# Second mixer of a two-block transformer: attention by head pairs at longer distances, masks on TensorE, two result banks, the whole convolution on VectorE, the output product begun early

## The chip, the core and the metric

The kernel runs on one core of a Trainium2 chip, in one launch. The metric is the time of one execution on the device in microseconds, the median over several runs. [...]

## The reference, cut to what matters

T = 256 rows, D = 1024. A first block of two layers (feed-forward, a mixer of three kinds of attention, feed-forward) is unchanged in what it computes. Behind it come two layers of this:

```
def hybrid_layer(x, ...):
    h = rms_norm_2(x, norm_g)
    z = h @ w_in
    (fq, fk, fv, ff, f_gate, glu_in, c_gate,
     nq, nkc, nvc, nks, nvs, nkw, nvw, n_gl, n_gate) = jnp.split(z, split_points, axis=-1)
    o_a = fox_attention(heads(fq, FOX_HEADS), heads(fk, FOX_HEADS),
                        heads(fv, FOX_HEADS), ff + fox_b) * jax.nn.silu(f_gate)
    o_b = conformer_conv(glu_in, conv_w, conv_b, conv_ln_g, conv_ln_b,
                         conv_pw) * jax.nn.silu(c_gate)
    o_c = nsa_attention(heads(nq, NSA_HEADS), ...) * jax.nn.silu(n_gate)
    mixed = jnp.concatenate([o_a, o_b, o_c], axis=-1)
    return x + mixed @ w_out
```

`fox_attention` has 4 heads of 64 with a decay on the scores (a running sum of log-sigmoids of `ff`). `conformer_conv` gates 256 channels by a sigmoid, runs a causal convolution of 31 taps on each channel, a layer norm over channels, a Silu and a 256 x 256 product. `nsa_attention` has 8 query heads on 2 key groups and three branches: compressed keys (15 blocks, each the result of a small network with a Gelu), selected keys and window keys; at T = 256 the selected and the window branch are both plain causal attention, with their own keys and values. The last layer is followed by a norm.

## The kernel before, in words

**Products.** A fp32 product is three products of rounded halves: with `whi`, `wlo` the high and the low part of a weight and `hh`, `hl` those of the normed input, `mm3` issues the three on PE at L301, L302 and L303. Other products and score terms go through `mm` (L306), transposes through `tr` (L311). A class `Stream` brings the weights in the order of a plan, a chunk of 128 x 1024 at a time: DMA into one of four `raw` buffers, ACT rounds it to `whi` (L261), DVE subtracts to get `wlo` (L265), both issued when the chunk's place among the split buffers comes free.

**Banks.** The eight PSUM banks are given out by rings: MM (0 to 2) for projections, SB (3, 4) for scores, TB (5, 6) for transposes, OB (7) for the sum over values, WB (0 to 4 and 7) for row products.

**A layer of the second mixer** (`mixer2`, L1108; layer 1 at 1337.8 to 1560.3 us of the trace, layer 2 from 1560.3 us on):
- Three row products of the input, each over eight 128-row slices of the depth: `nq`, `nkv` (512 columns) and `n3` (284 columns: fox values and small gates); then a rotation on DVE and `turn_n` (transposes of queries and keys, split into `qTh`, `qTl`, `kTh`, `kTl`).
- `weave(side(), 100, main, 44)` (L1647) interleaves two generators on one instruction stream. `main` is `tiles()`: pairs of 128-column tiles of the projection ("col2", 24 products of 256 columns a tile) and the compression product `bank<-raw,bl`, in the order glu, compressed keys and values, fox queries and keys, compression, gates. `side` is the attention, 32 heads-by-branches of nsa and then 8 of fox, with small work in between: branch gates, fox decay, layer norm, `compressed()`, `gating()`.
- Attention takes heads two at a time for the scores (`scores_pair`, run by `run_pairs`): three or four products into a bank, then for each head a custom DVE instruction (L695) that adds the causal table, writes the scores to `wk` and keeps their least value, and an Exp on ACT (L326). Each head is then turned by transposes, copied to SBUF alternately by DVE (L323) and ACT (L314), and multiplied with the values into the single OB bank. After 8 heads `fin_nsa` scales that bank on DVE into `oc` (directly, or through `ntmp` and an addition).
- The convolution: channels 0 to 127 on POOL (`conv_pool`, a scale L334 and an addition L329 a tap), channels 128 to 255 on DVE (`conv_dve`, L337, one `scalar_tensor_tensor` a tap).
- Gates: six column tiles times the row norms into `rg` on DVE, one Silu pass late (`gating`), which multiplies the turned results into `hh`, `hl`; then `out_rows`, the output product with `w_out` over all of `hh`, `hl`, four banks, and the residual addition.

What sets the order on each engine is the order in which these generators are advanced; every engine then works through its own list in that order, waiting at each entry for its semaphores.

## Time and profile before

| what | value |
|---|---|
| median of 3 runs | 1780.35 us (1779.28 to 1781.01) |
| profiled execution | 1780.6 us |
| its span | 1778.8 us |
| PE busy | 1654.0 us, 93% |
| DVE busy | 988.1 us, 56% |
| ACT busy | 807.5 us, 45% |
| POOL busy | 222.8 us, 13% |
| second mixer, layer 1 | 222.5 us |
| second mixer, layer 2 and final norm | 218.5 us |

The profiled execution is 0.25 us above the median and its span 1.8 us shorter than its time. PE busy is close to the span in the first block; the two layers of the second mixer are the last 441 us. "Busy" adds up the durations of instructions, and matmuls overlap in them, so the share of a stage is to be read with the idle time and the clock beside it.

### The profile page before, as it was taken

What the parts mean: (1) busy time and instruction counts of PE and PEld (TensorE: products, weight loads), DVE (VectorE), ACT (ScalarE), POOL (GpSimd) and SP (SyncE); (2) the same over time, 40 slices, a digit from 0 to 9 for tenths busy, and PEclk for the clock granted to TensorE, in tenths of its full rate; (3) what the DMA queues carried; (4) which work ended last, traced back from release to release, by engine and by line L of the source; (5) the groups of instructions that cost most, each with busy time, mean ns of one, the idle gap of its engine ahead of it and who ended that gap; (6) DMA issues with size and microseconds to landing.
All of it is one profiled execution on the core that took longest, in us unless ns stands there. A gap on an engine that the chain in (4) does not pass through costs nothing.

```text
span 1778.8 us, 24856 instructions
## 1 busy us (share of the span) xinstructions
PE 1654.0 (93%) x9598; PEld 1440.0 (81%) x9598; DVE 988.1 (56%) x1532; ACT 807.5 (45%) x1270; POOL 222.8 (13%) x298
## 2 busy tenths in 40 slices
PE   7999989999899999999999998999998779897796
PEld 6888889999788887888899998788877758686585
DVE  5554554445655546554654447555556755567564
ACT  5443444434454435443454444444435434454343
POOL 0000012212100000000112212000011620007200
PEclk9999999999999999999999999999999889898897
DMA  7555554333465555555454333555544132251421
GB/s 254 190 189 178 207 177 149 125 125 119 153 201 187 180 178 190 189 185 184 151 191 138 121 129 130 187 192 187 180 160 164 68 132 76 96 168 60 143 77 48
DMA packets 76582, 273.88 MB, mean 154 GB/s; under 512 B 8496, under 2 KB 9520, under 8 KB 76336
## 3 DMA queue, kind: packets, MB, share of 16 engines
q1 hardware_dynamic: 76464, 272.30, 45.7%
q8 instruction: 76, 1.25, 0.3%
q14 instruction: 42, 0.34, 0.1%
HBM read 271.21 MB, written 1.05 MB: 153 GB/s over the span
## 4 chain that ended last, share of the span: by engine, by line
PE 81%; DVE 9%; ACT 5%; issue 3%; DMA 1%; POOL 1%; DVEq 0%; SPq 0%; POOLq 0%; ACTq 0%
PE bank L301 24%; PE bank L303 23%; PE bank L302 23%; PE bank L306 8%; PE bank L311 4%; DVE wlo L265 2%; ACT whi L261 2%; ACT wk L326 1%; DMA raw<-W 1%; DVE wk L329 1%; POOL wk L329 1%; DVE cv L337 1%; ACT hh L314 1%; ACT L326 0%; DVE wk L695 0%
## 5 line engine op out<-in xcount | busy, mean ns | idle before, releaser
L265 DVE TENSOR_TENSOR wlo<-raw,whi 128x1024 fp32r<-128x1024 f32 (+5 forms) x468 | 566.2, 1213 | 502.2 <-ACT whi L261 483.9
L261 ACT ACTIVATE whi<-raw 128x1024 fp32r<-128x1024 f32 (+2 forms) x496 | 509.6, 1031 | 453.1 <-PE bank L303 437.1
L301 PE MATMUL bank<-whi,hh 128*128 128x512 f32 (+4 forms) x1120 | 421.6, 376 | 19.5 <-DVE wlo L265 11.9
L302 PE MATMUL bank<-wlo,hh 128*128 128x512 f32 (+4 forms) x1120 | 417.0, 372 | 0.0
L303 PE MATMUL bank<-whi,hl 128*128 128x512 f32 (+4 forms) x1120 | 416.9, 372 | 0.0
L301 PE MATMUL bank<-hh,whi 128*128 128x256 f32 x960 | 296.4, 309 | 0.0
L302 PE MATMUL bank<-hl,whi 128*128 128x256 f32 x960 | 275.9, 287 | 0.0
L303 PE MATMUL bank<-hh,wlo 128*128 128x256 f32 x960 | 275.8, 287 | 0.0
L301 PEld LDWEIGHTS bank<-whi,hh 128*128 128x128 f32 x1120 | 213.8, 191 | 57.5 <-issue 13.4
L303 PEld LDWEIGHTS bank<-whi,hl 128*128 128x128 f32 x1120 | 213.3, 190 | 33.6
L302 PEld LDWEIGHTS bank<-wlo,hh 128*128 128x128 f32 x1120 | 213.9, 191 | 32.2
L301 PEld LDWEIGHTS bank<-hh,whi 128*128 128x128 f32 x960 | 188.4, 196 | 7.1 <-issue 4.6
L302 PEld LDWEIGHTS bank<-hl,whi 128*128 128x128 f32 x960 | 188.6, 196 | 0.2
L303 PEld LDWEIGHTS bank<-hh,wlo 128*128 128x128 f32 x960 | 187.7, 196 | 0.0
L326 ACT ACTIVATE wk<-wk,nmt 128x128 f32<-128x128 f32 (+3 forms) x144 | 70.0, 486 | 213.4 <-DVE nmt L673 110.5
L303 PE MATMUL bank<-whi,gl 128*128 128x512 f32 x352 | 140.2, 398 | 0.0
L301 PE MATMUL bank<-whi,gh 128*128 128x512 f32 x352 | 138.8, 394 | 0.0
L302 PE MATMUL bank<-wlo,gh 128*128 128x512 f32 x352 | 138.7, 394 | 0.0
L329 POOL TENSOR_TENSOR stat<-stat 128x1 f32<-128x1 f32 x24 | 6.1, 259 | 941.7 <-ACT wk L326 941.2
L311 PE MATMUL bank<-kc,wk 128*128 128x128 f32 x580 | 98.7, 280 | 15.2 <-DVE wk L329 15.2
L265 POOL TENSOR_TENSOR wlo<-raw,whi 128x1024 fp32r<-128x1024 f32 x28 | 67.4, 2408 | 293.1 <-ACT whi L261 258.0
L311 PEld LDWEIGHTS bank<-kc,wk 128*128 128x128 f32 x580 | 71.4, 145 | 30.4 <-DVE wk L329 11.0
(247 smaller groups left out, 1773.3 us busy)
## 6 DMA issues: line engine op xcount, KB each, us to landing
raw<-W SPq DMA_DIRECT2D x464, 512.0 KB, 3.3
raw<-W SPq DMA_DIRECT2D x26, 384.0 KB, 3.4
gbc<-gains SPq DMA_DIRECT2D x10, 512.0 KB, 5.0
raw<-W SPq DMA_DIRECT2D x8, 416.0 KB, 3.1
tab<-tab SPq DMA_DIRECT2D x1, 2304.0 KB, 10.4
raw<-W SPq DMA_DIRECT2D x4, 426.0 KB, 3.5
raw<-W SPq DMA_DIRECT2D x6, 192.0 KB, 2.9
x<-x_in SPq DMA_DIRECT2D x2, 512.0 KB, 5.8
```

What stands on the lines that cost most here:

```text
L261: high = act.op(lambda e: e.activation(whi[i][:, 0:w], r[:, 0:w], ACT.Copy), self.landed[c], free)
L265: low = (low or dve).op(lambda e: e.tensor_tensor(wlo[i][:, 0:w], r[:, 0:w], whi[i][:, 0:w].bitcast(F), ALU.subtract), self.landed[c], hig ...
L301: pe.op(lambda e: e.matmul(dst, ah, bh, start=start, stop=False), *tokens, mark=False)
L302: pe.op(lambda e: e.matmul(dst, ah, bl, start=False, stop=False), mark=False)
L303: return pe.op(lambda e: e.matmul(dst, al, bh, start=False, stop=stop), mark=mark)
L306: return pe.op(lambda e: e.matmul(dst, a, b, start=start, stop=stop), *tokens, mark=mark)
L311: return pe.op(lambda e: e.transpose(dst, src, idn), *tokens, mark=mark)
L314: return act.op(lambda e: e.activation(dst, src, ACT.Copy), *tokens)
L326: return act.op(lambda e: e.activation(dst, src, f, **kw), *tokens)
L329: return eng.op(lambda e: e.tensor_tensor(dst, a, b, o), *tokens)
L337: return dve.op(lambda e: e.scalar_tensor_tensor(out=dst, in0=a, scalar=s, in1=b, op0=o1, op1=o2), *tokens)
```

## The change

The change rewrites `mixer2` and touches the weight stream.

- **Order of weights.** The glu tiles come right behind `nq`, ahead of `nkv` and `n3`. The fox keys come behind the compression product. The nsa and fox gates are row products ("ng", 512 columns, "fg", 256 columns) instead of six column tiles.
- **Stream.** The subtraction for `wlo` is owed and is issued by `st.lows()` half a tile later than its `whi`. This holds for the whole kernel; outside the second mixer it changes the place of DVE instructions only in the branch stage of the first mixer.
- **Attention.** 20 pairs of heads. The mask is a product on PE, `idr` x `hide` (128 x 256 columns); one `tensor_reduce` on DVE gives the least score of both heads; the two Exps read the bank directly. A pair is turned two pairs after its scores and its values follow one pair later; the copy of a turned pair is on DVE in one case of three, else on ACT. Sums over values alternate between banks 7 and 2.
- **Convolution.** All 62 taps on DVE, none on POOL: 3 for each chunk of `nkv`, 2 for each of `n3` and each part of `turn_n`, then one at every tick (three ticks a pair) until they are used up.
- **Layer norm, gates, output.** The variance's power is on POOL for one value a row, the reciprocal of 128 x 256 on DVE is gone; Silu is applied by ACT directly to the banks of "ng" and "fg"; gated results go to `qTh`, `ysh` and `hh`; the output product has banks of its own (EB: 0, 1, 3, 4), and its first four chunks are issued while the last pairs are turned. The second addition in `fin_nsa` is on POOL.
- Tiles of the second mixer are allocated and their zeros set once for both layers.

```diff
         rows("nq", "w_in_2", l, range(8), [(NQ + h * 64, 64) for h in NQ_HEADS], 2)
+        for c in [GA, GB, GA + 128, GB + 128]:
+            cols("col2", "w_in_2", l, 8, c)
         rows("nkv", "w_in_2", l, range(8), [(NKS, 128), (NKW, 128), (NVS, 128), (NVW, 128)], 2)
         rows("n3", "w_in_2", l, range(8), [(FV, 256), (FFG, 4), (NGL, 24)], 3)
-        for c in [GA, GB, GA + 128, GB + 128, NKC, NVC, FQ, FQ + 128, FK, FK + 128]:
+        for c in [NKC, NVC, FQ, FQ + 128]:
             cols("col2", "w_in_2", l, 8, c)
         for name in ("cmp_k_w1_2", "cmp_v_w1_2"):
             rows("cmp", name, l, range(16), [(0, 256)], 4)
-        for c in [FG, FG + 128, CG, CG + 128, NG, NG + 128, NG + 256, NG + 384]:
+        for c in [FK, FK + 128, CG, CG + 128]:
             cols("col2", "w_in_2", l, 8, c)
+        rows("ng", "w_in_2", l, range(8), [(NG, 512)], 2)
+        rows("fg", "w_in_2", l, range(8), [(FG, 256)], 4)
         rows("pw", "conv_pw_2", l, range(2), [(0, 256)], 2)
         rows("out", "w_out_2", l, OUT2, [(0, 1024)], 1)
     return plan
...
-                self.parts[c] = [high, low]
-                self.raw_free[c] = [high, low]
-                self.fetch()
+
+                def later():
+                    tok = (low or dve).op(lambda e: e.tensor_tensor(wlo[i][:, 0:w], r[:, 0:w],
+                                                                    whi[i][:, 0:w].bitcast(F), ALU.subtract),
+                                          self.landed[c], high, free)
+                    self.parts[c] = [high, tok]
+                    self.raw_free[c] = [high, tok]
+                    self.fetch()
+
+                self.owed.append(later)
+
+            def lows(self):
+
+                while self.owed:
+                    self.owed.pop(0)()
 
             def ahead(self, n, low=None):
 
                 while n and self.split < len(widths) and self.split - NSPLIT in self.done_tok:
...
+            for w in row_group("nkv", 8, 2, 512, H, norm.ready,
+                               take_rows("nkv", lambda t: ntm[:, t, 512:1024], 512), ring=WB):
+                some_taps(3)
+                yield w
...
+            def scores(u):
+                n = 128 * (u["t"] + 1)
+                i, bank, free = SB.take()
+                dst = bank[:, 0:2 * n].rearrange("p (a b) -> p a b", a=2)
+                (a, b), rest = u["terms"][0], u["terms"][1:]
+                mm(dst, a, b, True, False, free, u["ready"], base)
+                mm(dst[:, :, n - 128:n], idr[:, :], hide2, False, False, idr_tok)
+                for z, (a, b) in enumerate(rest):
+                    tok = mm(dst, a, b, False, z == len(rest) - 1, mark=(z == len(rest) - 1))
+                nm = nm_pair()
+                least = dve.op(lambda e: e.tensor_reduce(nm, dst, AX, ALU.min), tok)
+                u["i"], buf, sfree = sring.take()
+                u["buf"] = buf
+                for q in range(2):
+                    d = u["den"][q]
+                    u["exp"] = a_fn(buf[:, q * n:(q + 1) * n], bank[:, q * n:(q + 1) * n], ACT.Exp, least, tok, sfree,
+                                    base, scale=-1.0, bias=nm[:, q:q + 1], accum_out=sm[:, d:d + 1])
+                u["group"]["last"]["exp"] = u["exp"]
+                SB.give(i, u["exp"])
...
-                weave(side(), 100, main, 44)
...
+            sring = Ring([wk[:, z * 512:(z + 1) * 512] for z in range(3)], free=[free_w] * 3)
+            pring = Ring([wk[:, z * 512:(z + 1) * 512] for z in range(3, 6)], free=[free_w] * 3)
+            sides = [iter_chain(branch_gates(), decay(), compressed(), nsa_out()),
+                     iter_chain(taps, layer_norm(), conv_out())]
+            ending = out_rows("out", 8, lhs, mixed, lambda t: (1.0, None), after, OUT2, EB)
+            early = limited(ending, 4)
+            owed = [0.0]
+
+            def tick(rate):
+                owed[0] += rate
+                while owed[0] >= 1:
+                    owed[0] -= 1
+                    next(main, None)
+                for z in sides:
+                    next(z, None)
+
+            todo, n = pairs(), 20
+            made_ = []
+            for i in range(n + 3):
+                if i == n:
+                    drain(main)
+                    for z in sides:
+                        drain(z)
+                if i < n:
+                    made_.append(next(todo))
+                    scores(made_[i])
+                    tick(26 / 58)
+                for at, f in ((i - 2, turn), (i - 3, values)):
+                    if i < n:
+                        tick(26 / 58)
+                    else:
+                        next(early, None)
+                    if 0 <= at < n:
+                        f(made_[at])
+                yield
+            drain(fox_out())
+            Norm.xn_free = [toks["v_read"]] * 2
+            yield from ending
+            region[0] = h_last()
```

**Where instructions stand now, first place: DVE behind the first attention pairs.** Before, in layer 1, after the first nsa group (the `oc` row is its scaling) and the products of the compressed keys and values (`xT`):

```order
L329 TENSOR_TENSOR sm<-n_1,tab 128x8
L337 SCALAR_TENSOR_TENSOR sm<-sm 128x8
L1410 RECIPROCAL sm<-sm 128x8
L329 TENSOR_TENSOR sm<-sm 128x8
L329 TENSOR_TENSOR oc<-bank,sm 128x512
L329 TENSOR_TENSOR xT_1<-bank,rsb 64x128 x8
L695 ISA wk,nmt<-bank,kc 128x128
L695 ISA nmt 128x1
L695 ISA wk,nmt<-bank,kc 128x128
L695 ISA nmt 128x1
L329 TENSOR_TENSOR bl_1<-xT_1,tab 128x240 x4
L265 TENSOR_TENSOR wlo_0<-raw_0,whi_0 128x1024
```

Now, in the same stage of the same layer, from the tiles of the compressed keys and values on (L1462 is the one reduction of a pair, L359 on `cv` a tap):

```order
L1462 TENSOR_REDUCE nmt<-bank 128x2
L359 SCALAR_TENSOR_TENSOR cv<-yp,tab,cv 128x256
L355 TENSOR_SCALAR sm<-sm 128x48
L1240 RECIPROCAL sm<-sm 128x48
L359 SCALAR_TENSOR_TENSOR cv<-yp,tab,cv 128x256
L351 TENSOR_TENSOR bl_0<-xT_0,tab 128x240 x4
L351 TENSOR_TENSOR sm<-n_0,tab 128x8
L359 SCALAR_TENSOR_TENSOR sm<-sm 128x8
L359 SCALAR_TENSOR_TENSOR cv<-yp,tab,cv 128x256
L1462 TENSOR_REDUCE nmt<-bank 128x2
L359 SCALAR_TENSOR_TENSOR cv<-yp,tab,cv 128x256
L355 TENSOR_SCALAR sm<-sm 128x8 x2
```

The two custom passes with their read-outs became one reduction of `bank`, and between each reduction and the next there are now taps, the four additions into `bl`, and small steps of the branch gates and the decay. The scaling of the first group (`oc`) moved to a later place.

**Second place: ACT around the Silus.** Before, where the Silus of the convolution and of the gates stood, behind the last Exp:

```order
L326 ACTIVATE cw_0<-cw_0 128x120 [waits s_dve]
L314 ACTIVATE wk_0<-bank5 128x256 [waits s_pe]
L314 ACTIVATE cw_0<-bank6 120x128 [waits s_pe]
L326 ACT_TABLE_LOAD
L326 ACTIVATE cv_0<-cv_0,tab_0 128x256
L326 ACTIVATE cv_0<-cv_0,tab_0 128x256 [waits s_act]
L326 ACTIVATE rg_0<-rg_0 128x1024 [waits s_dve]
L326 ACTIVATE rg_0<-rg_0 128x1024
L314 ACTIVATE hh_0<-glu_0 128x512 [waits s_dve] x2
```

Now, between the Exp of one fox pair (bank 3) and that of the next (bank 4); `rgn` is the nsa gate read from banks 1 and 0 of the product "ng":

```order
L348 ACTIVATE wk_0,sm_0<-bank3,nmt_0 128x256
L348 ACT_TABLE_LOAD [waits s_act]
L348 ACTIVATE rgn_0<-bank1,stat_0 128x512 [waits s_act]
L348 ACTIVATE rgn_0<-bank0,stat_0 128x512
L348 ACTIVATE rgc_0<-rgc_0 128x512
L269 ACTIVATE whi2_0<-raw2_0 128x1024 [waits s_raw2]
L348 ACTIVATE cv_0<-cv_0,tab_0 128x256 x2
L336 ACTIVATE ysh_0<-cv_0 128x512 [waits s_act]
L336 ACTIVATE wk_0<-bank6 128x256 [waits s_pe]
L336 ACTIVATE qTh_0<-bank5 128x4x128 [waits s_pe]
L348 ACT_TABLE_LOAD [waits s_pe]
L348 ACTIVATE wk_0,sm_0<-bank4,nmt_0 128x256 [waits s_dve]
```

The Silus moved ahead of the Exps of the last pairs, and a table load stands on either side of them.

**Third place: PE at the key transposes of the compressed branch.** Before (bank 6 is a TB bank, the `kcv,tab` product the one that spreads the compressed values):

```order
L301 MATMUL bank0<-hh_0,whi0_0 128x256
L302 MATMUL bank0<-hl_0,whi0_0 128x256
L303 MATMUL bank0<-hh_0,wlo0_0 128x256
L306 MATMUL bank6<-kcv_0,tab_0 120x128 [waits s_dve]
L306 MATMUL bank7<-ntm_0,wk_0 128x64 x2
L306 MATMUL bank7<-ntm_0,wk_0 128x64 [waits s_act]
L306 MATMUL bank7<-ntm_0,wk_0 128x64
L301 MATMUL bank4<-kch_0,qTh_0 128x32
```

Now:

```order
L325 MATMUL bank0<-hh_0,wlo0_0 128x256
L333 MATMUL bank6<-kc_0,kcv_0 128x15 [waits s_dve]
L328 MATMUL bank5<-kcv_0,tab_0 120x128
L333 MATMUL bank6<-kc_0,wk_0 128x128 [waits s_dve]
L333 MATMUL bank6<-kc_0,wk_0 128x128 x3
L323 MATMUL bank0<-hh_0,whi0_0 128x256
```

The transpose of the compressed keys (`bank6<-kc_0,kcv_0`), the value product and the transposes of a pair of heads stand directly behind each other now, and the pair's transposes (`kc_0,wk_0`) wait for a DVE instruction, since they take bank 6 again.

## Rows read from the trace of the kernel before

**Rows 1.** Windows: start:end, us, busy (instructions) of five engines, PEclk, DMA share, GB/s.

```profile
1337.80:1560.30 222.50, 185.89 (x1099) 157.87 (x1099) 139.21 (x300) 98.57 (x200) 51.33 (x83) 0.89 0.33 109
1560.30:1778.80 218.50, 175.19 (x1065) 149.12 (x1065) 132.64 (x295) 93.78 (x196) 45.24 (x68) 0.90 0.28 96
...
1583.30:1591.50 8.20, 4.73 (x39) 4.28 (x38) 5.81 (x10) 6.29 (x10) 0.00 (x0) 1.00 0.64 198
...
1608.80:1660.00 51.20, 34.97 (x201) 29.64 (x200) 41.41 (x92) 18.57 (x47) 42.91 (x61) 0.83 0.13 43
...
1744.60:1774.30 29.70, 26.54 (x112) 22.15 (x112) 14.65 (x20) 9.22 (x16) 1.11 (x2) 0.90 0.15 54
```

**Rows 2.** Waits of PE, 1560 to 1779 us: total us, times, longest.

```profile
PE bank L306 <- DVE wk L323: 10.3, 4, 5.1
PE bank L306 <- DVE oc L329: 9.8, 2, 5.5
PE bank L301 <- DVE ysl L329: 5.3, 1, 5.3
PE bank L306 <- DVE ntmp L329: 3.7, 1, 3.7
```

**Rows 3.** Timeline, PE, by start: us, engine line, operation, count, idle before.

```profile
1606.15 0.28 PE L301 MATMUL bank<-hh,whi 128*128 128x256 f32 x1
1606.27 0.28 PE L302 MATMUL bank<-hl,whi 128*128 128x256 f32 x1
```

**Rows 4.** Timeline, PE, 512-column products of nq.

```profile
1568.13 0.39 PE L302 MATMUL bank<-wlo,hh 128*128 128x512 f32 x1
1568.35 0.39 PE L303 MATMUL bank<-whi,hl 128*128 128x512 f32 x1
```

**Rows 5.** Timeline, PE, one wait for the bank of values.

```profile
1616.53 0.41 PE L306 MATMUL bank<-ntm,wk 128*128 128x64 f32 x2 [4.31 <-DVE oc L329]
```

**Rows 6.** Lines by form, DVE, 1557 to 1779 us: count, busy us, mean ns, idle before.

```profile
L337 DVE SCALAR_TENSOR_TENSOR cv<-yp,tab,cv 128x256 f32<-128x256 f32 x30 | 19.4, 647 | 0.7
L695 DVE CUSTOM_DVE_ANT_0 wk<-bank,kc 128x256 f32<-128x256 f32 x20 | 7.7, 420 | 15.1 <-PE bank L306 15.1
L695 DVE CUSTOM_DVE_ANT_0 wk<-bank,kc 128x128 f32<-128x128 f32 x20 | 4.9, 283 | 2.4 <-PE bank L306 2.2
L323 DVE COPY wk<-bank 128x256 f32<-128x256 f32 x10 | 4.2, 419 | 0.7 <-PE bank L311 0.7
L329 DVE TENSOR_TENSOR rg<-bank,rsb 128x512 f32<-128x512 f32 x6 | 4.1, 687 | 3.9 <-PE bank L303 3.9
...
L329 DVE TENSOR_TENSOR bl<-xT,tab 128x240 f32<-128x240 f32 x4 | 3.1, 841 | 0.0
...
L1580 DVE RECIPROCAL glu<-glu 128x256 f32<-128x256 f32 x1 | 1.7, 1741 | 0.0
...
L329 DVE TENSOR_TENSOR wk<-ntm,kc 128x192 f32<-128x192 f32 x4 | 1.2, 352 | 0.2 <-ACT ntm L317 0.2
```

**Rows 7.** Timeline, DVE: a tap and a wlo, POOL idle.

```profile
1671.82 1.23 DVE L265 TENSOR_TENSOR wlo<-raw,whi 128x1024 fp32r<-128x1024 f32 x1 [2.23 <-ACT whi L261]
1672.96 1.00 DVE L337 SCALAR_TENSOR_TENSOR cv<-yp,tab,cv 128x256 f32<-128x256 f32 x2
```

**Rows 8.** Timeline, DVE: four taps, POOL in its convolution.

```profile
1640.97 2.83 DVE L337 SCALAR_TENSOR_TENSOR cv<-yp,tab,cv 128x256 f32<-128x256 f32 x4
```

**Rows 9.** Timeline, ACT: the Exp of one head, a weight's high half.

```profile
1700.05 0.51 ACT L326 ACTIVATE wk<-wk,nmt 128x256 f32<-128x256 f32 x1 [2.79 <-DVE nmt L695]
...
1701.05 1.04 ACT L261 ACTIVATE whi<-raw 128x1024 fp32r<-128x1024 f32 x1
```

**Rows 10.** Timeline, ACT: the table load of the Silus.

```profile
1735.38 1.28 ACT L326 ACT_TABLE_LOAD   x1
1736.67 1.23 ACT L326 ACTIVATE cv<-cv,tab 128x256 f32<-128x256 f32 x2
```

**Rows 11.** Timeline, DVE, branch stage of the first mixer.

```profile
446.71 1.75 DVE L265 TENSOR_TENSOR wlo<-raw,whi 128x1024 fp32r<-128x1024 f32 x1
```

## The prediction on record

> **What bounds the kernel now.** I read the windows first, since the change stays in the two layers of the second mixer. Layers 1 and 2 take 222.5 and 218.5 us, 441.0 together, of a span of 1778.8 (1780.6 with the 1.8 around it, 0.25 above the median) [rows 1]. In layer 2 PE is busy 175.19 us, more than DVE (132.64) or ACT (93.78) [rows 1]. PE is thus the bound, but idle for 43.3 us, of which 4.5 are the final norm behind 1774.3. The waits of PE say whom it waits for: DVE everywhere. 10.3 us for copies of turned heads, 9.8 and 3.7 for `oc` and `ntmp`, the scalings that free the only bank of values, 5.3 for `ysl` of the convolution; with eleven kinds in all 36 us [rows 2]. One of them is plain in the timeline: the values product that starts at 1616.53 stood idle for 4.31 us behind `oc` [rows 5]. The third cost is the clock: mean granted 0.90 over the layer, 1.00 in 1583.3 to 1591.5 and 0.83 in 1608.8 to 1660, where most of the long waits lie [rows 1]. At a half clock in some 20% of 218.5 us, 44 us, with PE busy some 0.6 of it, about 13 us are lost. So layer 2 without its tail is 214.0 = 165 of work at full clock + 36 of waits + 13 of slow clock.
>
> **Work of PE.** At full clock a 256-column product follows the last by 0.12 us [rows 3], a 512-column one by 0.22 to 0.23 [rows 4]. Added a layer: 20 masks of 256 columns, 20 x 0.12 = 2.4. The nsa gates as a row product are 48 x 0.227 = 10.9 instead of four column tiles, 96 x 0.12 = 11.4: -0.5. The fox gates are 48 products of 256 columns either way. The variance by rows saves some 0.8. Sum +1.1, work 166. The early start of the output product adds none; it fills waits.
>
> **Load of DVE and ACT.** A tap is 0.46 us while POOL is idle (two in 1.00, less their overlap) [rows 7], and 0.71 while POOL convolves (four in 2.83) [rows 8]; on the average 0.647 [rows 6]. So 61 taps cost 28.1 instead of 19.4 for 30: +8.7. Gone are 40 custom passes (7.7 + 4.9 and their read-outs, some 3.3); in their place 20 reductions of 256 or 512 columns, priced like the copy of 256 (0.42) and the product of 512 (0.69) [rows 6], 11.1: -4.8. I bound a reduction by 0.42 and 1.5, as the latter no row excludes, and take the former pair, because every plain pass over a bank in [rows 6] runs near one column a nanosecond. At the upper end a layer's DVE gains 13 us. Fewer copies -3.3, three gates by ACT -2.1, the reciprocal of 1.74 -1.7 [rows 6], an addition to POOL -1.4 (at about 1 us there, hidden: POOL is idle). DVE stays near 128 of 200 us: enough on the average, so what matters is the order in its queue. The 20 pairs' Exps at 0.5 a head [rows 9] are unchanged; ACT takes over copies and Silus, to some 100. The later place of `wlo` costs nothing where DVE has slack: in the first mixer's branches DVE runs without a gap, 1.75 for a `wlo` [rows 11], but it has the same work in another order, covered by PE; if that cover failed it were at most one 1.75 a phase, 3.5 in all. Memsets (1 us each on POOL, once instead of twice) are hidden.
>
> **Waits of PE, walked along the new order, per layer.** The waits of [rows 2] for copies, banks of values and `ysl` should mostly go: a copy has two pairs' work ahead of its use, a bank of values is one of two, the convolution is done before the pairs end. Late next are these:
> - turn_n behind 26 taps: the four `nkv` chunks give 2.7 us of PE each (12 x 0.227) and 1.23 + 3 x 0.46 = 2.6 on DVE, then come the rotation (four at 0.35, two more) [rows 6], the scalings, and three `n3` chunks of about 2.2 with 1.9 on DVE. DVE is some 4 to 5 behind: 4.5 us. Queued behind are `qTl` and `kTl`, for which the first scores wait.
> - the decay product waits for `ls`, behind four `bl` additions (0.84 each beside POOL [rows 6], 0.7 without it by the ratio of the taps), a table load of 1.28 for the Ln [rows 10], and two taps: 5.0.
> - bank 6: the pair's transposes wait for the split of the compressed keys, which is behind a `whi` (1.04), two Exps (1.0) [rows 9], and a `wlo` (1.23) and a tap on DVE: 4.5. Behind it on PE stands the next projection, which everything follows.
> - the fox gate product waits for bank 1, read by the first Silu of "ng" behind its table load: 1.28 + 0.8 + a wait for the `whi` or Exp ahead, 1.4: 3.5.
> - `oc` times its gate and the table change around the product "pw": 3.5.
> - hidden transposes behind Gelu 2.0, a copy behind the split fox queries 1.5, `oa` at the end 1.5, others 1.5: 6.5.
>
> Sum 27.5 instead of 36. **Clock:** all of these are 5 us or less and lie apart; in 1583.3 to 1591.5 PE was idle for 3.5 of 8.2 us at a clock of 1.00 [rows 1], so short waits need not cost clock. Bounds 0 and the present ratio, 13/36 = 0.36 of the waits; I take 0.2: 5.5. Layer without tail: 166 + 27.5 + 5.5 = 199 instead of 214.0, -15.0. Layer 1 has the same order and the same waits, so -30 in all: 1780.6 - 30 = 1750.6, say **1750 us**.
>
> **A rule weighed against a row.** A table load is 1.28 us, and the Silu starts 0.01 us after it ended (1735.38 + 1.28, next 1736.67) [rows 10], so a load costs 1.3 on ACT. The Trainium skill ("ScalarE: Activation LUTs", What ACT_TABLE_LOAD costs) puts a drain of about 1.38 us on top, 2.66 a switch, and its next section advises grouping by table set, which speaks against Silus between Exps. By the page the two switches at the gates would cost 2.8 us more a layer, an estimate, and the result would be near 1756; the trace here shows no such drain.
>
> **Rivals.**
> - *The lag does not build up.* DVE has over 70 us a layer to spare, and if it enters `n3` on time, and the splits of `kcl` and `ls` pass ACT's and DVE's queues at once, waits are 13 and clock 2.6: 181.6 a layer, -32.4, 1716 us. For it: in row 7 DVE idles 2.23 before the `wlo` [rows 7]. Against: DVE is in order, and the taps are put ahead of what PE waits for. Chance 0.27.
> - *New waits for old.* 36 us of waits at other places, the same clock: 166 + 36 + 13 = 215, 1783 at the old ratio, 1780 with the output product's start filling a little. For it: every wait of [rows 2] was on DVE, and DVE's load falls by only 4. It is also where the change does not do what it says. Chance 0.12.
> - *DVE's queue becomes the bound, slower.* In each of the first 12 pairs the reduction, with the pair's Exps behind it, stands behind three taps and a `wlo`, 3 x 0.46 + 1.23 = 2.6 us. If PE cannot run ahead in each of them, that is 31 a layer, of which 9.5 (the first two waits above) are counted: waits 49, clock 17.6, layer 232.6, +37, 1817 us. It decides from waits of 35.5 a layer on (166 + 1.36 x 35.5 = 214), 8 more than mine, so once seven of twelve pairs pay in full. For it: before, taps stood one or two at a time between heads, and PE still waited 10.3 us for copies [rows 2]. Against: a pair is used two pairs later. Chance 0.11. The Trainium skill ("TensorE: Matmul & The Clock Gate", Architectural detail) has the queues of ScalarE and VectorE as strict first-in first-out, as the order of starts in the trace agrees; by that rule no reduction passes a tap.
>
> **How the numbers follow.** My case has 0.50, with waits of 18 to 34 and clock of 3 to 9: 187 to 209 a layer, 1727 to 1771. Range: down to 1706 for waits of 10 and clock 1 (the 0.27 reach below 1716 with about a quarter), up to 1778, which leaves out the slower case and half of the 0.12: 0.07 + 0.11 + 0.05. A measurement of this kernel tells apart about 0.2%, 3.6 us. Faster: 0.49 + 0.27 + 0.03 = 0.79. Within: 0.01 + 0.05 = 0.06. Slower: 0.11 + 0.04 = 0.15.
>
> **What would show it.** Right: the waits of PE for value copies, `oc` and `ntmp` under 3 us together; a tap at 0.46 throughout; POOL near 0; PE idle before the first `kTh` product, the `ls` product and bank 6, by 4 to 5 each; the clock over 0.93 in the attention. Wrong: a reduction that takes over 1 us, PE waiting for Exps in every pair, a clock that stays at 0.83, or an output product that waits in its early chunks.

## The result, and the profile after

| | before | changed |
|---|---|---|
| median | 1780.31 us (8 runs, 1777.14 to 1782.65) | 1770.18 us (8 runs, 1765.06 to 1776.63) |
| ratio | | 0.9947, 95% interval 0.9928 to 0.9966 |
| profiled span | 1778.8 us | 1769.2 us |

The kernel is 10 us faster, 0.53%. The forecast was 30, with a range of 1706 to 1778: the sign and the range held, the size did not. Executions of the changed kernel lie in two groups, six of the eight at 1765 to 1772 us (granted clock 0.976 to 0.981) and two near 1777 (0.967), so medians of such kernels that differ by less than some 4 us are not told apart.

The page of the changed kernel, part 1 (busy time of each engine; PE is TensorE and PEld its weight loads, DVE VectorE, ACT ScalarE, POOL GpSimd):

```profile
PE 1655.8 (94%) x9554; PEld 1438.6 (81%) x9554; DVE 970.5 (55%) x1427; ACT 802.6 (45%) x1263; POOL 138.5 (8%) x174
```

POOL lost its 84 us, as it should; PE is as busy as before. The windows of the two layers of the second mixer (columns as in [rows 1]; layer 1 is counted from the end of the last long wait of the first block, here and for the other kernels below):

```profile
1334.50:1553.90 219.40, 186.38 (x1082) 156.40 (x1082) 130.98 (x248) 96.45 (x197) 7.85 (x17) 0.91 0.33 112
1553.90:1769.20 215.30, 176.21 (x1043) 148.12 (x1043) 123.09 (x242) 91.33 (x192) 5.49 (x9) 0.93 0.29 98
```

Before, that wait ended at 1336.7, so counted the same way the layers took 223.6 and 218.5. They gained 4.2 and 3.2 us, and the second mixer begins 2.2 earlier; d3 below shows which edit these came from. The waits of PE in layer 2 of the changed kernel (total us, times, longest):

```profile
PE bank L328 <- DVE ls L351: 4.8, 1, 4.8
PE bank L333 <- DVE kcl L351: 4.2, 1, 4.2
PE bank L323 <- ACT rgn L348: 3.9, 1, 3.9
PE bank L323 <- DVE ntm L342: 3.1, 1, 3.1
PE bank L333 <- DVE oc L351: 2.5, 1, 2.5
PE bank L333 <- DVE oa L351: 2.2, 2, 1.3
PE bank L333 <- ACT hidr L348: 2.1, 1, 2.1
PE bank L333 <- DVE qTl L359: 1.8, 1, 1.8
PE bank L323 <- ACT rgf L348: 1.7, 1, 1.7
PE bank L328 <- ACT wk L348: 1.6, 1, 1.6
```

The waits of [rows 2] are gone: none for copies of turned heads over 0.7, none for `ntmp`. In their place stands what the walk had found: 4.8 for `ls` (forecast 5.0), 4.2 for `kcl` (4.5), 3.9 for `rgn` (3.5), 2.5 and 1.7 around `oc` and the pw product (3.5), 2.1 for the hidden units (2.0), and 1.8, 0.6 and 1.6 at turn_n (4.5). One was not on the list: 3.1 for `ntm`, where the glu products now take bank 0, which still holds `nq`. With small ones the waits of layer 2 sum to 32.1 us instead of 36.0.

The last piece is the clock. Windows of 10 us in layer 2, each from the end of one wait, in the changed kernel (behind 3.06 us for `ntm`, 4.77 for `ls`, 2.08 for the hidden units, 4.24 for `kcl`, 3.93 for `rgn`, and behind 2.46 and 1.74 for `oc` and pw; PEclk is the first number behind the busy times):

```profile
1564.20:1574.20 10.00, 9.99 (x71) 10.00 (x72) 3.34 (x4) 2.12 (x2) 0.00 (x0) 0.83 0.43 153
1616.80:1626.80 10.00, 9.82 (x49) 6.89 (x50) 6.12 (x16) 5.22 (x15) 0.00 (x0) 0.84 0.17 54
1650.00:1660.00 10.00, 9.60 (x67) 8.58 (x67) 6.99 (x20) 3.53 (x8) 0.27 (x1) 0.83 0.33 120
1663.90:1673.90 10.00, 9.60 (x62) 9.05 (x63) 6.51 (x15) 4.25 (x10) 0.00 (x0) 0.83 0.17 54
1712.30:1722.30 10.00, 9.96 (x67) 9.59 (x67) 4.69 (x8) 7.29 (x14) 1.29 (x1) 0.84 0.14 54
1727.80:1737.80 10.00, 9.95 (x44) 8.61 (x44) 4.91 (x6) 4.48 (x7) 0.00 (x0) 0.76 0.27 79
```

The first five have 0.83 or 0.84: a third of the 10 us at 1.2 GHz instead of 2.4, some 1.6 us of work lost, behind a wait of 2.08 as behind one of 4.77. In layer 1 four of the same five waits show 0.80 to 0.84, but the one of 3.06 us 0.70, so the price is not fixed:

```profile
1347.60:1357.60 10.00, 9.98 (x61) 10.00 (x62) 3.51 (x6) 2.12 (x2) 0.00 (x0) 0.70 0.35 127
```

The same windows in the kernel before, behind its six waits of 3.1 to 5.5 us, are these:

```profile
1616.50:1626.50 10.00, 5.66 (x33) 5.46 (x33) 9.64 (x22) 3.11 (x6) 8.91 (x13) 0.83 0.21 72
1627.30:1637.30 10.00, 10.00 (x65) 9.71 (x66) 7.63 (x17) 4.38 (x11) 8.83 (x14) 0.83 0.00 0
1641.10:1651.10 10.00, 8.02 (x43) 6.54 (x43) 7.08 (x14) 4.09 (x12) 8.83 (x14) 0.83 0.10 30
1652.80:1662.80 10.00, 9.95 (x39) 5.70 (x40) 5.45 (x12) 1.48 (x5) 4.19 (x6) 0.73 0.19 62
1686.40:1696.40 10.00, 10.00 (x57) 9.43 (x57) 2.76 (x7) 5.19 (x10) 0.00 (x0) 0.70 0.11 41
1744.60:1754.60 10.00, 9.99 (x40) 8.78 (x41) 6.35 (x7) 3.37 (x5) 0.00 (x0) 0.71 0.21 60
```

Ten times what is missing to 1.00 sums to 13.7 us before and to 10.7 now, with another 1.7 behind the last two waits for `oa`, of 1.3 and 0.9 us (0.83): 12.4. Two more windows of the kernel before belong beside these. Behind its wait of 2.1 us for `kTh` the clock stayed full, and around the wait for `ysl`, which began at 1739.3, it was already down 2.6 us earlier, so the 13.7 is about 1 too low:

```profile
1591.20:1601.20 10.00, 10.00 (x84) 9.83 (x84) 5.39 (x19) 5.11 (x17) 0.00 (x0) 1.00 0.31 107
1736.60:1750.40 13.80, 7.75 (x30) 6.87 (x31) 7.15 (x10) 6.62 (x11) 0.00 (x0) 0.51 0.13 39
```

The waits became shorter, but not fewer, and the clock's part of layer 2 fell by only some 2 us.

### The profile page after: what moved, and what is told of

Read it like the earlier page. It is cut to its first block, busy times and chain, and to the rows that moved or that the text cites. A ratio compares the mean times of both kernels' runs of the same rounds, so it can differ in the third digit from the quotient of the medians.

```text
span 1769.2 us, 24549 instructions
## 1 busy us (share of the span) xinstructions
PE 1655.8 (94%) x9554; PEld 1438.6 (81%) x9554; DVE 970.5 (55%) x1427; ACT 802.6 (45%) x1263; POOL 138.5 (8%) x174
## 4 chain that ended last, share of the span: by engine, by line
PE 80%; DVE 8%; ACT 5%; issue 3%; POOL 1%; DMA 1%; DVEq 0%; SPq 0%; POOLq 0%; ACTq 0%
PE bank L323 23%; PE bank L325 23%; PE bank L324 23%; PE bank L328 8%; PE bank L333 4%; DVE wlo L275 2%; ACT wk L348 2%; ACT whi L269 1%; DVE cv L359 1%; POOL wk L351 1%; DVE wk L351 1%; ACT L348 1%; DMA raw<-W 1%; DVE nmt L1462 1%; ACT hh L336 0%
## 5 line engine op out<-in xcount | busy, mean ns | idle before, releaser
L275 DVE TENSOR_TENSOR wlo<-raw,whi 128x1024 fp32r<-128x1024 f32 (+3 forms) x468 | 565.6, 1212 | 509.5 <-ACT whi L269 478.2
L269 ACT ACTIVATE whi<-raw 128x1024 fp32r<-128x1024 f32 (+4 forms) x496 | 509.6, 1032 | 460.7 <-PE bank L325 444.8
L323 PE MATMUL bank<-hh,whi 128*128 128x256 f32 x864 | 265.0, 307 | 6.1 <-DVE ntm L342 6.1
L324 PE MATMUL bank<-hl,whi 128*128 128x256 f32 x864 | 247.8, 287 | 0.0
L325 PE MATMUL bank<-hh,wlo 128*128 128x256 f32 x864 | 247.8, 287 | 0.0
L323 PEld LDWEIGHTS bank<-hh,whi 128*128 128x128 f32 x864 | 169.7, 196 | 13.7 <-issue 11.2
L324 PEld LDWEIGHTS bank<-hl,whi 128*128 128x128 f32 x864 | 169.4, 196 | 0.7
L325 PEld LDWEIGHTS bank<-hh,wlo 128*128 128x128 f32 x864 | 168.5, 195 | 0.0
L348 ACT ACTIVATE wk<-wk,nmt 128x128 f32<-128x128 f32 (+3 forms) x64 | 34.2, 535 | 110.2 <-DVE nmt L701 110.2
L324 PEld LDWEIGHTS bank<-wlo,gh 128*128 128x128 f32 x352 | 66.5, 189 | 16.7
```

The costliest lines, as they stand in the source:

```text
L269: high = act.op(lambda e: e.activation(whi[i][:, 0:w], r[:, 0:w], ACT.Copy), self.landed[c], free)
L275: tok = (low or dve).op(lambda e: e.tensor_tensor(wlo[i][:, 0:w], r[:, 0:w], whi[i][:, 0:w].bitcast(F), ALU.subtract), self.landed[c], hig ...
L323: pe.op(lambda e: e.matmul(dst, ah, bh, start=start, stop=False), *tokens, mark=False)
L324: pe.op(lambda e: e.matmul(dst, ah, bl, start=False, stop=False), mark=False)
L325: return pe.op(lambda e: e.matmul(dst, al, bh, start=False, stop=stop), mark=mark)
L348: return act.op(lambda e: e.activation(dst, src, f, **kw), *tokens)
```

## Experiments

Each kernel ran beside the kernel before on the same chip. Times are medians; in brackets the ratio to before with its interval.

### Undoing one part

**u1, one bank for the sums over values.**

```diff
-            for at in (..., [0, 1], [7, 2], [0, 1, 3, 4]))
+            for at in (..., [0, 1], [7], [0, 1, 3, 4]))
```

> The changed kernel with one bank (7) for the sums over values instead of two. Theory A (a group's scaling has a pair's time, some 8 us, before the next group's first values product, since the pairs are spaced by three ticks of main work): the second bank gains nothing, 1770 within 4 us, no wait of PE for oc or the scaled temporary over 1 us. Rival B (the single bank was what cost 9.8 and 3.7 us of waits a layer before): these waits return, and with the clock behind them the time is 1790 to 1805.

1768.91 us (0.9946, 0.9930 to 0.9963). Nothing changes; the waits for `oc` are the same 2.5 at the transposes and 0.3 elsewhere. The second bank is worth nothing here: the waits of 9.8 and 3.7 are gone without it. The spacing of the pairs is the likely reason; it was not tried apart from the rest of the new order.

**u2, short distances.**

```diff
-                for at, f in ((i - 2, turn), (i - 3, values)):
+                for at, f in ((i - 1, turn), (i - 2, values)):
```

> The changed kernel with a pair turned one pair after its scores instead of two, and its values one pair later again; nothing else. Theory A (a pair is 8 to 9 us of work, and reduction, Exps and copy take under 5): no new wait over 2 us, 1770 within 5. Rival B (the longer distance is what removed the 10.3 us of waits a layer for copied heads): they come back at each late Exp, with slow clock behind each, 1785 to 1800.

1770.95 us (0.9948, 0.9936 to 0.9960). No change either, as long as `ls` and the start of the attention stop PE anyway.

**u3, half of the convolution on POOL.**

```diff
+                for j in range(1, 31):
+                    m_ = ts(pool, tmp, yp[:, 0, j:j + 256], w[:, j:j + 1], 1.0, ALU.mult, ALU.mult, sp_)
+                    sp_ = tt(pool, acc, acc, tmp, ALU.add, m_, sp_)
...
-                     iter_chain(taps, layer_norm(), conv_out())]
+                     iter_chain(taps, pause(31), layer_norm(), conv_out())]
```

> The changed kernel with channels 0 to 127 convolved on POOL as before (a scale and an addition a tap), 31 taps on DVE, the layer norm 31 ticks later, and the second addition of the nsa scaling back on DVE. Theory A (what PE waits for on DVE is one instruction behind a few others, not DVE's total load): the wait for ls shrinks by a tap or two only, DVE's instructions beside POOL take 0.2 to 0.45 longer each, sum within 6 of 1770. Rival B (DVE's load is the bound of the attention stage): 14 us of taps a layer less give waits some 5 us a layer shorter, 1755 to 1762. Rival C (the contention with POOL was a large part of the time before): 1778 to 1790.

1796.36 us (1.0099, 1.0083 to 1.0115), 26 more than the changed kernel; rival C by its sign, and twice its size. In the groups of DVE by form, in the first 75 us of layer 2, a tap is as dear as before the change, the rotation's products take 0.54 instead of 0.35 [rows 6] and the additions into `bl` 0.86 instead of 0.59 in the changed kernel:

```profile
L359 DVE SCALAR_TENSOR_TENSOR cv<-yp,tab,cv 128x256 f32<-128x256 f32 x30 | 19.6, 655 | 0.6
...
L351 DVE TENSOR_TENSOR wk<-ntm,kc 128x192 f32<-128x192 f32 x4 | 1.9, 539 | 0.0
```

30 taps take 19.6 us beside POOL, where the changed kernel has 60 taps in 26.7. All of DVE is busy for 125.1 us in layer 2, against 123.1 in the changed kernel: its load did not fall, but rotation, splits and `bl`, which PE waits for, became slower, in a stage in which POOL did not work before the change. PE waits for them (the same view as above, both layers; the changed kernel has 9.5 for `ls` and none for this `ntm`):

```profile
PE bank L328 <- DVE ls L351: 12.9, 2, 7.2
...
PE bank L333 <- DVE ntm L351: 8.3, 2, 4.1
```

**u4, the low halves at once.**

```diff
-                self.owed.append(later)
+                later()
```

> The changed kernel with wlo issued at once behind its whi, as before the change, everywhere. Theory A: the changed kernel's layer 1 of the second mixer started 2.7 us earlier than that of before, and this is the only edit ahead of it, so those 2.7 come back: 1772 to 1774, and more waits of about 1 us in the second mixer. Rival B: the 2.7 us are scatter between executions; 1770 within 2.

1780.38 us (1.0007, 0.9992 to 1.0021): the whole gain is gone, more than either theory said. The one edit that I had costed at nothing carries 10 us. Its runs lie between 1777 and 1788, the profiled one at the upper end; that one shows one wait that grew by much, from 2.08 to 5.01:

```profile
1441.72 0.63 PE L333 MATMUL bank<-kc,hidr 30*128 30x30 f32 x4 [5.01 <-ACT hidr L348]
```

On DVE it shows why: the pair's reduction (L1462) stands behind three taps and two `wlo`, the first of which waited 2.10 us for its `whi`. The scores were complete at 1435.1.

```profile
1434.56 1.23 DVE L275 TENSOR_TENSOR wlo<-raw,whi 128x1024 fp32r<-128x1024 f32 x1 [2.10 <-ACT whi L269]
1435.71 0.88 DVE L359 SCALAR_TENSOR_TENSOR cv<-yp,tab,cv 128x256 f32<-128x256 f32 x2
1436.50 1.22 DVE L275 TENSOR_TENSOR wlo<-raw,whi 128x1024 fp32r<-128x1024 f32 x1
1437.63 0.48 DVE L359 SCALAR_TENSOR_TENSOR cv<-yp,tab,cv 128x256 f32<-128x256 f32 x1
1438.03 0.68 DVE L1462 TENSOR_REDUCE nmt<-bank 128x2 f32<-128x512 f32 x1
```

This wait is only a part of the price. All waits of both layers sum to 70.1 us here and to 66.9 in the changed kernel, but the layers take 448.2 instead of 434.7, and the mean clock is lower:

```profile
1337.80:1563.90 226.10, 191.77 (x1082) 161.59 (x1082) 131.37 (x248) 96.57 (x197) 7.87 (x17) 0.89 0.33 109
1563.90:1786.00 222.10, 181.66 (x1043) 153.84 (x1043) 123.41 (x242) 91.37 (x192) 5.48 (x9) 0.89 0.28 95
```

Most of the 13.5 us is thus clock, in an execution 7 us above the median; why so little waiting brings so much of it is not shown. The edit also moves the request for the next weights, but in neither kernel does PE wait for a DMA in these layers.

**d3, the kernel before with this edit alone.** The stream and its callers as in the change, `mixer2` as before.

> The kernel before with only the stream's edit: wlo owed and issued half a tile behind whi, everywhere. The changed kernel without this edit was as slow as the one before. Theory E (the edit helps any order, since DVE no longer stands waiting for a whi with a reduction behind it): 1765 to 1772, the whole gain of the change. Rival F (it helps only with the new order, where a pair's one reduction stands behind it): 1778 to 1781. The first block alone, where layer 1 of the second mixer began 2.7 us earlier, gives 1777.

1769.63 us (0.9933, 0.9921 to 0.9945), as fast as the changed kernel: theory E. A part of the gain lies in the first mixer's branch stage. Its waits of PE there in layer 1, kernel before:

```profile
PE bank L301 <- DVE wk L329: 5.8, 3, 3.7
```
and in d3:

```profile
PE bank L315 <- DVE wk L343: 3.7, 1, 3.7
```

2.1 us in two waits, in each of the first block's layers, and the clock behind them; the second mixer began at 1330.9 in d3 and at 1334.5 in the changed kernel (before 1336.7). Over the eighteen profiled kernels with this edit, which do the same work up to there, it began between 1330.9 and 1338.0, at 1333.8 on the average, so some 3 us of the gain lie ahead of it and the 5.8 of d3 are a favourable case. The rest lies in the second mixer:

```profile
1330.90:1551.40 220.50, 185.51 (x1104) 158.20 (x1104) 140.33 (x301) 99.12 (x201) 51.33 (x83) 0.89 0.34 112
1551.40:1766.70 215.30, 173.82 (x1065) 148.99 (x1065) 132.19 (x295) 93.61 (x196) 45.13 (x68) 0.92 0.29 98
```

220.5 and 215.3, against 219.4 and 215.3 in the changed kernel and 223.6 and 218.5 before. The waits of PE account for 4 of these 6.3 us, 70.9 instead of 74.9, and the mean clock of layer 2 rose from 0.90 to 0.92. The rewritten mixer is worth at most 1 us.

### Taking waits away, one by one

**f1, glu products into banks 7 and 4.**

```diff
+        GB2 = Ring(banks, [7, 4], bank_free)
...
-                yield from col_pair("col2", H, norm.ready, take_glu(n), M2)
+                yield from col_pair("col2", H, norm.ready, take_glu(n), GB2)
```

> The changed kernel, the two glu products into banks 7 and 4 instead of 0 and 1, which nq still holds. It takes away one wait of 3.06 us a layer, behind which the trace shows 1.5 to 2.8 us lost to half clock. Theory A (each wait of 2 us or more brings its own stretch of half clock, whatever its length): -2 x (3.06 + about 2) = -10, 1760. Rival B (clock is lost in proportion to the time waited, 0.2): -7.3, 1763. Rival C (the wait moves on: the scaling of nq is late on DVE and the next reader waits as long): 1770 within 3.

1763.24 us (0.9906, 0.9893 to 0.9919), 7 less, rival B's figure, though the 3 us between A and B are within the scatter. The clock is 1.00 where the wait was.

**f2, the decay product later.**

```diff
-                yield
+                yield from pause(4)
                 i, bank, free = M2.take()
                 for t in range(2):
                     tok = mm(bank[:, 0:256], ls[:, t, :], tri[:, t, :], t == 0, t == 1, d6, free, mark=(t == 1))
```

> The changed kernel with the decay's running-sum product (the one that waited 4.8 us for ls) issued four ticks later; its result is used only by the fox pairs. Theory A: -2 x (4.8 + 0.6 of half clock) = -11, 1759. Rival C (DVE is behind at this place whatever PE waits for, so the next scores or copy wait instead): above 1766, and a wait of 2 to 4 us on the next instruction that needs DVE.

1762.06 us (0.9906, 0.9893 to 0.9919), 8 less. This lies between A and rival C. Of 4.8 us, 2.4 stayed, as 1.28 for the next pair's Exp and 1.17 for `ls`. Both are short, and yet the 10 us behind them show

```profile
1615.50:1625.50 10.00, 9.98 (x46) 6.07 (x47) 7.95 (x21) 6.37 (x21) 0.00 (x0) 0.85 0.31 96
```

so in this execution, of 1766 us, the edit removed waiting and gave back no clock.

**f3, compressed keys and values in one transpose bank.** The product with `rep` moves ahead of the transpose, into columns 128 on of the same bank.

> The changed kernel with the transpose of the compressed keys and the product of the compressed values in one transpose bank, so that the pair's transposes behind them take the other. It takes away the wait of 4.24 us for kcl, and 1.2 of half clock behind it: theory A -2 x 5.4 = -11, 1759. Rival C (the pair's transposes after next wait for the same bank, and the compressed scores for kcl): above 1766.

1769.30 us (0.9941, 0.9929 to 0.9952). Rival C: the 4.24 us for `kcl` became 3.15 for `vbd`, the other reader of that bank, behind the same ACT and DVE work.

**f4, gates out of their banks by DVE.** `v_scaled` into `rgn` and `rgf`, Silu in place behind it.

> The changed kernel with the products ng and fg scaled out of their banks by DVE (0.7 and 0.4 us an instruction), and Silu applied in place on ACT later, so that no bank waits for ACT's table load. It takes away the waits of 3.93 and 1.74 us a layer and up to 1.5 and 2.0 of half clock behind them. Theory A: -2 x 5.7 of waits and -2 x 1.5 to 3.5 of clock, -14 to -18, 1752 to 1756. Rival C (DVE's scalings stand behind wlo and reductions and are as late as ACT's): above 1764.

1770.93 us (0.9947, 0.9931 to 0.9964). Rival C: instead of 3.93, 2.46 and 1.74 there are now 1.53, 2.75, 1.62 and 1.52; nothing gained.

**d2, taps late.** No `some_taps` ahead of the attention, two taps a tick in it.

> The changed kernel with no tap ahead of the first attention pair, and two taps at every tick instead of one, for about as many pairs. Theory A (26 taps ahead of the pairs make DVE late at the end of n3: waits 1.8, 0.6 and 1.6): these waits go, but each reduction has six taps between it and the next, 2.7 us, with scores waiting in turn: 1770 to 1780. Rival D (the taps beside the reductions cost nothing, as DVE idles for 2 to 4 us in every pair): 1760 to 1764.

1770.74 us (0.9944, 0.9933 to 0.9956). The waits at turn_n went, `ls` grew from 4.8 to 6.0. Moving the taps is worth nothing by itself.

**d1, a longer wait.** Ten DVE copies ahead of `ls`.

> The changed kernel with ten DVE copies of 256 columns (0.42 us each, of the convolution's padded input into an unused buffer) put ahead of ls in each layer, so that the wait for ls grows from 4.8 to about 9. Theory A (half clock comes once for a wait, whatever its length): +4.2 a layer and no more than 0.5 of clock, 1778 to 1779; the stretch of half clock behind it stays under 3 us. Rival B (clock lost in proportion to the wait): +4.2 x 1.3, 1781 or more.

1774.94 us (0.9964, 0.9951 to 0.9977), about 5 more. The wait grew by less than planned; in layer 2 it is now

```profile
1622.66 2.07 PE L328 MATMUL bank<-tab,ls 128*128 128x256 f32 x4 [7.56 <-DVE ls L351]
```
and the 10 us behind it

```profile
1622.70:1632.70 10.00, 9.82 (x48) 7.05 (x48) 5.85 (x15) 3.22 (x10) 0.00 (x0) 0.81 0.17 53
```

2.8 us more of waiting in each layer, and a clock of 0.81 instead of 0.84. Two times 2.8 is 5.6, so the waits alone account for the time, as in theory A. Loss of clock in proportion to the wait would have shown 0.75.

### All of them together

**c2.** f1, f2, f4, and f3 with its next step four ticks on; hidden transposes two ticks later; the gated nsa result one tick ahead of its transposes; pw in a transpose bank; `fox_out` in pieces between the early chunks and the first held chunks of the output product:

```diff
+                    if (i, f) in ((n + 1, values), (n + 2, turn)):
+                        next(fo)
                 yield
-            drain(fox_out())
+            next(fo)
             Norm.xn_free = [toks["v_read"]] * 2
+            next(ending)
+            next(fo)
```

> The changed kernel with every wait of PE over 1.5 us attacked: glu products in banks 7 and 4; decay product four ticks later; compressed keys and values in one transpose bank and the next step four ticks on; hidden transposes two ticks later; gates scaled out of their banks by DVE; gated nsa result one tick before its transposes; the pw product in a transpose bank; the gated fox results spread over the early chunks and the first held chunks of the output product. Theory A (time is PE's work plus its waits plus about 1.5 us of half clock for each wait over 2 us): waits fall from 32 to 10 or less a layer, clock from 10 to 3, so 1770 - 2 x 29 = 1712, to 1725 if a third of the waits come back elsewhere. Rival C (PE keeps the same distance to DVE and ACT, waits only move): 1750 or more.

1740.05 us (0.9770, 0.9759 to 0.9782), 30 less than the changed kernel; between theory A's 1725 and rival C's 1750. The waits of PE of both layers fell from 66.9 to 47.3 us, 19.6, so each microsecond of waiting gave back 1.5. This kernel has more edits than the four single ones, whose two gains sum to 15, and they were not taken apart. What is left is again DVE and ACT at their queues' heads. In c2, the row that makes PE wait 3.38 us for the compressed copy (`kcv`), and what stood ahead of it:

```profile
1629.82 0.68 DVE L1467 TENSOR_REDUCE nmt<-bank 128x2 f32<-128x512 f32 x1
1632.61 1.23 DVE L276 TENSOR_TENSOR wlo<-raw,whi 128x1024 fp32r<-128x1024 f32 x1 [2.10 <-ACT whi L270]
1633.75 0.40 DVE L346 COPY kcv<-bank 15x256 f32<-15x256 f32 x1
```
and on ACT

```profile
1630.54 0.47 ACT L349 ACTIVATE wk<-bank,nmt 128x256 f32<-128x256 f32 x1 [2.59 <-DVE nmt L1467]
...
1631.45 1.05 ACT L270 ACTIVATE whi<-raw 128x1024 fp32r<-128x1024 f32 x1
```

The reduction ends at 1630.5, two Exps and a `whi` follow on ACT, and DVE stands still for 2.10 us at the `wlo` of that `whi`, although the copy behind it could run: the product that it reads was done at 1628.8.

**g1 and g2, the low half of a column tile a whole tile behind,** in the changed kernel and in c2.

```diff
                 if k == nk // 2 - 1:
-                    st.lows()
                     yield None
```

> The changed kernel with the wlo of column tiles issued a whole tile behind their whi instead of half a tile. Theory G (a wlo at the head of DVE's queue, waiting for a whi behind the pair's Exps, makes the instruction behind it 2 us late, and PE with it): the waits for kcl, oc and ls shrink by about 2 us each, 3 to 6 us a layer, 1758 to 1765. Rival H (DVE has too much to do there, order aside): 1768 to 1772.

> The version with the waits removed (1740) and the same edit. Theory G: its waits for the compressed copy (3.4), the weights of the compressed branch (3.7) and the gated result (3.7) shrink by about 2 each, and a wait that falls under 2 us loses its stretch of half clock: 1722 to 1732. Rival H: 1738 to 1742.

g1: 1770.30 us (0.9944, 0.9925 to 0.9962), nothing in the median. Its eight runs lie between 1764 and 1775. In the profiled one, of 1764, `kcl` fell from 4.24 to 3.10 and `ls` in one layer from 4.8 to 3.2, `rgn` and `oc` did not move, and all waits of both layers sum to 59.4 instead of 66.9; a gain of a few microseconds is thus possible and not shown. g2: 1726.89 us (0.9705, 0.9692 to 0.9718), 13 less than c2; `kcv` is gone and `cw` fell from 3.7 to 1.5, while `oc` kept its 3.7. Theory G holds in c2, where few other waits are left; for the changed kernel its 1758 to 1765 did not come.

**n1, c2 without the masks.**

> The version with the waits removed, without the 20 mask products a layer; the attention is then not causal, nothing else is left out. By the trace they take 0.125 us each, 2.5 a layer. If PE's time is what is left (theory A), -5: 1735. If the time is set by what PE waits for (rival), 1740 within 2.

This kernel leaves the masks out, so its attention is not causal. 1734.22 us (0.9752, 0.9733 to 0.9770), 6 less, for two times 20 products, as in theory A. In c2 the product behind a mask starts 0.12 us after it on the average.

**c4, the best version.** c2 with g2's edit, d2's taps, and a tick more ahead of two transposes of the compressed branch.

> The version with the waits removed, and: the wlo of column tiles a tile later; one tick more ahead of the transposes of the compressed keys and of the compressed branch's weights; no tap ahead of the attention, two a tick in it. Theory A: of the 20 us of waits a layer that are left, 1.8 + 0.6 + 1.6 (late DVE at the end of n3) go with the taps, and 6 with the rest, and two to three stretches of half clock: 1740 - 2 x 13 = 1714 to 1722. Rival: two taps a tick make each reduction late, 1730 or more.

1720.13 us (0.9662, 0.9650 to 0.9675), 50 less than the changed kernel and 60 less than before, within theory A's range. The layers and the two largest waits:

```profile
1332.70:1527.80 195.10, 179.16 (x1081) 149.64 (x1082) 132.97 (x252) 95.82 (x195) 7.83 (x17) 0.95 0.39 126
1527.80:1719.60 191.80, 169.20 (x1043) 143.25 (x1043) 124.44 (x246) 90.55 (x190) 5.46 (x9) 0.95 0.33 110
```
```profile
PE bank L334 <- DVE oc L352: 7.4, 2, 3.7
PE bank L329 <- ACT wk L349: 4.4, 2, 2.2
```

The waits of the two layers sum to 33.9, 33 less than in the changed kernel: again 1.5 us of time for 1 of waiting.

**c5, the pw product ahead of the last nsa transposes,** in c4.

> The best version so far (1720) with the pw product issued ahead of the last transposes of the nsa result, which waited 3.7 us, instead of behind them. Theory A: the wait shrinks by the product's 1.4 us and its stretch of half clock may go, -3 to -6, 1714 to 1717. Rival C (the first early chunk of the output product needs the split of those transposes and now waits for it, about 1.5 us): 1719 to 1722.

1725.59 us (0.9696, 0.9682 to 0.9711), slower. The one wait of 3.72 became two, 3.21 ahead of pw (its bank) and 1.95 at the first early chunk. Worse than rival C.

**c6, c4 with one bank and short distances.**

> The best version so far (1720) with one bank for the sums over values and a pair turned one pair after its scores, its values one later, as in u1 and u2 together. Theory A (a pair is 8 us of work, so either has time enough): 1718 to 1724. Rival B (in the changed kernel other waits hid what they cost): 1730 or more, with waits of PE for wk or oc.

1724.99 us (0.9694, 0.9680 to 0.9708), 5 more. This misses theory A's range by 1 us; the wait for `wk` that rival B names appears, but not its 1730. In place of c4's 2.21 and 1.66 at the first pairs stands

```profile
1580.92 0.54 PE L334 MATMUL bank<-kc,wk 128*128 128x128 f32 x2 [3.55 <-ACT wk L349]
```

and the product of the layer norm waits 3.56 for the last tap instead of 1.57. The distances, the banks or both are worth some 5 us, but only once the rest is gone; the two were not tried apart.

## Why the prediction was wrong

- **Waits walked along the order, 27.5.** Measured 32.1. Every large named wait was there, within 1 us of its size; of the small ones the copy behind the split fox queries (1.5) hardly was. The step that failed is the list's completeness. The new reader of bank 0 behind `nq` (3.1) I had not walked, although the order shows the bank; small ones (`cw`, `oa`) made the rest.
- **Clock, 5.5.** The step "short waits need not cost clock", with 0.2 us for a microsecond of waiting, failed. By the windows 12.4 us of layer 2 are lost after the change, where I had 5.5. Nearly every wait had a stretch of half clock near it, worth some 1.6 us of work behind 2.1 us as behind 4.8 or 7.6 (d1), and twice that in one case. The upper bound that I gave, 0.36 of the waits, 10 to 11, would have been the better choice. The premise was not false, only weighed too high: the clock did stay full behind a wait of 1.8 and behind one of 2.1.
- **The later `wlo` "costs nothing", worth nothing.** The step that failed most. I asked what it could cost, not what it could give. u4 and d3 show that it is the whole gain, 10 to 11 us. Two places are seen where it stood in the way: ahead of the first mixer's gate products, and (u4) at DVE's head behind a `whi`. My own row for it, 1.75 us of `wlo` between the products that PE waits for [rows 11], was the place to see it.
- **The sum of -30** was thus made of the wrong parts: d3 and u4 put the rewritten mixer at 0 to -1 us where I had -30, and the stream's edit at -10 where I had 0. Against the layer of 199 that I forecast, layer 2 took 210.8 without its tail: waits 4.6 and clock 6.9 above the forecast, 11.5 of the 11.8 us. Against the 214.0 before, it gained 3.2 where I had 15.0, and d3 gains the same 3.2 there without the rewrite.
- **Work of PE, +1.1.** The product behind a mask starts 0.12 us after it, 2.5 a layer (forecast 2.4), and n1 gives 6 for both layers: right. The whole term is less sure. What is left of layer 2 when waits and clock are taken off is 163 to 164 before (214.0 - 36.0 - 13.7 to 14.7) and 166.3 after (210.8 - 32.1 - 12.4), so +2 to +3; an estimate, and no run separates it. The level of 166 was met, the start of 165 was 1 to 2 too high.
- **The rivals.** "New waits for old" was right for the mixer, and had 0.12; its 1780 is what u4 measures. "DVE's queue becomes the bound" was right in its mechanism (an instruction behind others at DVE's head) and wrong in place: not the taps, whose move in d2 changes nothing, but the `wlo` that waits for ACT. "The lag does not build up", 1716, is what c4 nearly reaches at 1720, with most of the waits that I listed removed and 17 left a layer.
- **The load of DVE,** 61 taps at 0.46: measured 0.475, the reductions 0.42 and 0.69 as chosen; DVE is busy 123 us in layer 2 (forecast 128) and ACT 91 (forecast 100). Near enough, and nothing hung on it. The upper end that I gave for DVE, 13 us more, comes to 14 by its own terms. The rule on table loads in the Trainium skill ("ScalarE: Activation LUTs", What ACT_TABLE_LOAD costs) would have added a drain of 1.38 us a switch. In the changed kernel, too, the next ACTIVATE starts 0.01 us after a load:

```profile
1710.16 1.28 ACT L348 ACT_TABLE_LOAD   x1
1711.45 1.26 ACT L348 ACTIVATE rgn<-bank,stat 128x512 f32<-128x512 f32 x2
```

## What to carry to other kernels

Count the waits of the engine that bounds the kernel, and do not only sum them: here a microsecond of waiting removed gave 1.5 us on the average, while a wait that only changed its length (d1) moved the time by no more than that length. Before rewriting a stage, look for an instruction that stands at the head of a queue waiting for another engine while ready work is behind it; moving that one instruction by half a tile gave 10 us, and the rewrite around it nothing more. When a rewrite moves the time little, list the waits of the new order and remove them together: of four single removals two gave 7 and 8 us and two nothing, since the wait came back at the next reader; these four with a few more gave 30 us.

## What was not expected of the hardware

The clock: behind single waits of 2.1, 3.1, 3.9, 4.2, 4.8 and 7.6 us the next 10 us show 0.81 to 0.84 in layer 2 (windows above), while it stayed at 1.00 in the 9.3 us behind a wait of 1.8:

```profile
1599.90:1609.20 9.30, 7.75 (x62) 7.35 (x62) 8.96 (x20) 2.85 (x5) 0.00 (x0) 1.00 0.27 95
```

The length of the wait does not decide it: the kernel before shows 1.00 behind one of 2.1, f2 shows 0.85 behind two of 1.2 to 1.3 close together, and the same wait of 3.06 us is followed by 0.83 in layer 2 and 0.70 in layer 1. What decides stays open. The Trainium skill ("TensorE: Matmul & The Clock Gate", HAM oscillation) describes a loop in which the fall of the clock is paid again at every interruption instead of once; the trace agrees for the six waits above, at about 1.6 us each, and not for those of 1.8 and 2.1.

And VectorE beside GpSimd: a tap of 256 columns 0.475 us alone and 0.655 with POOL convolving (u3), the rotation's products 0.35 and 0.54. The Trainium skill ("GPSIMD Engine Reference", Specifications) has the two engines share their interfaces to SBUF, with contention for VectorE's instructions of two SBUF inputs; a tap and the rotation's products are such, and both slowed. Taking 43 us of work a layer off an otherwise nearly idle engine was worth 26 us in this order. Why the runs of u4 scatter over 10 us stays open, as does the split of c2's gain among its edits.
